# A relative-bias scratch of 23 copies instead of 128, and its skewed read in the weights' queue

## The chip, the cores and the metric

The kernel runs on one core of a Trainium2 chip. The metric is the device time of one execution in microseconds; the median over the runs counts. TensorE (PE), VectorE (DVE), ScalarE (ACT) and GpSimd (POOL) compute, SyncE (SP) issues transfers, and 16 DMA engines move the data, whichever engine issued them.

## The reference, cut to what matters

Two transformer blocks run one behind the other on 256 tokens of width 1024, all in float32. The first block has two layers (mixer, memory cross-attention, convolutional feed-forward). The second has one layer, and its attention adds a bias that depends on the head and on the distance of query and key alone:

```python
d = jnp.maximum(dist, 0)                         # dist = query - key
large = max_exact + (jnp.log(df / max_exact) / math.log(...) * (REL_BUCKETS - max_exact)).astype(jnp.int32)
bucket = jnp.where(d < max_exact, d, jnp.minimum(large, REL_BUCKETS - 1))
...
bias_gr = rel_bias.T.reshape(G, R, REL_BUCKETS)
s_c = einsum("bgrqd,bgcd->bgrqc", qb, kc) + bias_gr[:, :, t5_bucket(tq[:, None] - cend[None, :])]
s_s = einsum("bgrqd,bgqld->bgrql", qb, k_sel) + bias_gr[gi5, ri5, t5_bucket(dist_s)[:, :, None]]
s_w = einsum("bgrqd,bgsd->bgrqs", qb, kwb) + bias_gr[:, :, t5_bucket(dist_w)]
```

There are 16 heads. Since only the distance counts, a head's bias over keys is the same row of numbers for each query, shifted by one place from query to query.

## The kernel before

**Weights.** Nearly all of the work is products with weights, which are read once. They lie in memory in the order of use, cut into pieces of up to 128 x 1024; two equal neighbours make a group (`grouped`), mostly 1024 KB. SyncE runs one loop over the groups (`sync`, L2343 to L2351): group `gi` goes into slot `gi % NR` of a ring of `NR` = 4, and its issue waits until the products have used all pieces of group `gi - 4` (`product`, "used"). ScalarE casts each piece to its high part (`highs`, L998), VectorE subtracts to get the low part (`lows_due`, L1494), both up to 3 pieces ahead of the product, in the order of their programs; TensorE then multiplies high and low parts (`run`, L477). So a group that lands late makes ScalarE wait, then VectorE, then TensorE.

**The first place: the write of the scratch.** While the feed-forward of the first block's first layer runs, TensorE and VectorE make the 16 heads' bias rows, 384 numbers each, in partitions 0 to 15 of `PT`. GpSimd then writes each row 128 times into the scratch `d_scr` in memory (L2276, behind the eighth of its 22 products of that stage). Its signal is `bias_out`.

**The second place: the skewed read.** Partition p of the table `TB` (128 partitions x 16 heads x 256 keys) needs a head's row from place 127 - p on. A step of 383 from one partition to the next, over copies that stand 384 apart, gives that shift. GpSimd issues the read (L2303, signal `bias_in`) once the first block's last operations no longer need the space of `TB` (`first_block_done`: the last normalisation, and the last of the products "dn"). VectorE is the only reader: first for the compressed keys (L2041), later for each unit of the attention.

**The weights around the second place.** The second block begins with two products for the queries ("q2", 0 and 1), then two for keys and values ("kv2", 0 and 1), 4 pieces each, so two groups each. The first of them is computed by row tile (`tokens_by_tile`): tile 0, then tile 1, and a piece counts as used only after tile 1. The groups of "kv2" 0 are issued when the groups of "q2" 0 are free, those of "kv2" 1 when the groups of "q2" 1 are.

Of the kernel before, what the change touches and what calls it, by code (L numbers as in the profile page):

```python
# [25 lines left out]
NR = 4  # L26
# [205 lines left out]
def build(nc, wstream, specs_out, cst_d, rel_d, par_d, par2_d, x_d, xT_d, memT_d, lnp_d, scr_d, out_d, layout):  # L232
    with ExitStack() as ctx:

        def sb(name, f):
            return ctx.enter_context(nc.sbuf_tensor(name, [128, f], F32))
# [4 lines left out]
        def signal(name, step=1):  # L241
            s = Signal(ctx.enter_context(nc.semaphore("s_" + name)), step)
            signals.append(s)
            return s
# [3 lines left out]
        product = signal("product")  # L248
# [4 lines left out]
        vec = signal("vec")  # L253
# [3 lines left out]
        cst_in, x_in, p2_in, rel_in, mem_in, bias_out, bias_in = (  # L257
            signal(n, 16) for n in ("cst", "x", "p2", "rel", "mem", "bias_out", "bias_in"))
# [16 lines left out]
        PT = sb("PT", 2048)  # L275
# [26 lines left out]
        def arena(n):  # L302
            o = at[0]
            at[0] += n
            assert at[0] <= ARENA
            return ar[:, o:o + n]
# [35 lines left out]
        def pr(name, p=128):  # L342
            o, n = layout["par"][0][name]
            return par[0:p, o:o + n]
# [11 lines left out]
        q2 = arena(2048).rearrange("p (f t) -> p f t", t=T)  # L356
        kT2 = arena(1024).rearrange("p (b f t) -> p b f t", b=2, t=T)
        TB_o = at[0]
        TB = arena(4096).rearrange("p (h s) -> p h s", s=T)
# [55 lines left out]
        pieces = Pieces()  # L415
# [1070 lines left out]
        def vector(e):  # L1486
            w = Waits(e)
# [538 lines left out]
            for i in range(2):  # L2026
# [5 lines left out]
                bc = TB[:, :, first:first + 16 * (ncv - 1) + 1:16]  # L2032
                b3 = A["csc", i][:, 0:240].rearrange("p (h c) -> p h c", c=NC15)
                w.wait_ge(cross, "csc", i)
                w.wait_ge(bias_in)
                if i:
                    w.wait_ge(cross, "pT2", 0, 6, 0)
                    w.wait_ge(cross, "pT2", 0, 7, 0)
# [153 lines left out]
        def gpsimd(e):  # L2192
            w = Waits(e)

            def inverse_root(dst, src, n=1, p=128):
                w.wait_ge(cst_in)
                return e.tensor_tensor(dst, src, mhalf[0:p, 0:n], ALU.pow)  # L2197
# [6 lines left out]
            def scaled(tag, *ready):  # L2204

                w.wait_ge(*ready)
                for i in range(2):
                    e.tensor_scalar(xt(i), xt(i), ALPHA, None, ALU.mult).then_inc(*pool.done("scaled", *tag, i))

            def roots(tag):  # L2210

                for i in range(2):
                    st, mv, nm, ve_, rs, nr = norm_smalls(i)
                    w.wait_ge(vec, "var", *tag, i)
                    inverse_root(rs, ve_).then_inc(*pool.done("rs", *tag, i))
# [6 lines left out]
            for l in range(DEPTH):  # L2222
                scaled((l, 1), *((x_in,) if l == 0 else (cross, "xT", 0, 3, 1, 1)))

                def rope_sin(br, i):
                    Xv = qk[:, i, 640 * br:640 * br + 640].rearrange("p (h s d) -> p h s d", s=2, d=32)
                    t2v = room[br][:, 640:1280].rearrange("p (h s d) -> p h s d", s=2, d=32)
                    n1 = rot[:, br, i, 32:64].unsqueeze(1).to_broadcast([128, 10, 32])
                    if i:
                        w.wait_ge(vec, "rope", l, br, 0)  # L2230
                    e.tensor_tensor(t2v[:, :, 0, :], Xv[:, :, 1, :], n1, ALU.mult).then_inc(*pool.done("sin", l, br, i))

                w.wait_ge(cst_in)
                if l:
                    for n in range(NZ - 4, NZ):
                        w.wait_ge(pool, "z", 0, n)
                        w.wait_ge(vec, "z", 0, n)
                for i in range(2):
                    w.wait_ge(act, "q", l, 0, i)
                    w.wait_ge(act, "k", l, i)  # L2240
                    rope_sin(0, i)
                for i in range(2):
                    w.wait_ge(vec, "vvar", l, i)
                    inverse_root(sm[:, 32 * i + 15:32 * i + 16], sm[:, 32 * i + 14:32 * i + 15]).then_inc(*pool.done("vrs", l, i))
                    w.wait_ge(vec, "qvar", l, i)
                    inverse_root(sm[:, 84:94], sm[:, 74:84], 10).then_inc(*pool.done("qrs", l, i))
                    if i == 0:
                        w.wait_ge(vec, "qg", l, 0)
                        rope_sin(1, 0)
                    w.wait_ge(act, "vn", l, i)  # L2250
                    w.wait_ge(par_in[l])
                    e.tensor_tensor(vt[:, i, :], vt[:, i, :], pr("clng"), ALU.mult).then_inc(*pool.done("vgain", l, i))
                    w.wait_ge(pool, "vgain", l, i)
                    e.tensor_tensor(vt[:, i, :], vt[:, i, :], pr("clnb"), ALU.add).then_inc(*pool.done("vn", l, i))
                w.wait_ge(vec, "qg", l, 1)
                rope_sin(1, 1)
                for kind, n, d in fills:
                    if kind == "merge" and n != 2:
                        w.wait_ge(vec, "mul", l, n, d)
                        w.wait_ge(*((vec, "mul", l, 2, d) if n == 0 else (pool, "merged", l, 0, d)))  # L2260
                        e.tensor_tensor(merged[:, d, :], merged[:, d, :], gates[:, gate_at[n] + d, :],  # L2261
                                        ALU.add).then_inc(*pool.done("merged", l, n, d))
                roots((l, 1))
                next_gains((l, 1), 3 * l + 1, (l, 2))
                scaled((l, 2), cross, "xT", l, 1, 1, 1)
                roots((l, 2))
                next_gains((l, 2), 3 * l + 2, (l, 3))
                scaled((l, 3), cross, "xT", l, 2, 1, 1)
                for n in range(NZ):
                    s = 2 * n % 8  # L2270
                    w.wait_ge(act, "ga", l, n)
                    w.wait_ge(vec, "conv", l, n + NZ)
                    e.tensor_tensor(hc[:, s, :], hc[:, s, :], hc[:, s + 1, :], ALU.mult).then_inc(*pool.done("z", l, n))  # L2273
                    if l == 0 and n == 7:
                        w.wait_ge(vec, "rel")
                        e.dma_start(scr_d, PT[0:16, 1024:1408].unsqueeze(1).to_broadcast([16, 128, 384])).then_inc(*bias_out.done())  # L2276
                if l == 0:
                    w.wait_ge(vec, "conv", 0, 2 * NZ - 1)
                    e.dma_start(par, par_d[1]).then_inc(*par_in[1].done())
                else:  # L2280
                    for n in range(NZ - 4, NZ):
                        w.wait_ge(pool, "z", 1, n)
                        w.wait_ge(vec, "z", 1, n)
                    e.dma_start(grow, lnp_d[6][:, 0:1024]).then_inc(*gain_in[2, 1].done())
                roots((l, 3))
                if l == 0:
                    next_gains((0, 3), 3, (1, 1))
# [4 lines left out]
                    w.wait_ge(vec, "rvar", *tag, i)  # L2292
                    inverse_root(rs, ve_).then_inc(*pool.done("rrs", *tag, i))

            def first_block_done():
                for i in range(2):
                    w.wait_ge(vec, "ln", 1, 3, i, 1)
                w.wait_ge(product, "dn", 1, 1, 1)

            rms((2, 1))  # L2300
            w.wait_ge(bias_out)
            first_block_done()
            e.dma_start(TB, bass.AP(scr_d.tensor, 127, [[383, 128], [128 * 384, 16], [1, 256]])).then_inc(*bias_in.done())  # L2303
            for i in range(2):
                w.wait_ge(vec, "qv", i)
                inverse_root(ve[i][:, 48:72], ve[i][:, 24:48], 24).then_inc(*pool.done("qrs2", i))
# [1 line left out]
            def keys_scaled(i):  # L2308
                Xh = qb[:, i, :].rearrange("p (h d) -> p h d", d=64)
                w.wait_ge(vec, "qsc", i)  # L2310
                w.wait_ge(p2_in)
                for h, name in ((16, "ksn"), (20, "kwn")):
                    e.tensor_tensor(Xh[:, h:h + 4], Xh[:, h:h + 4], p2(name).unsqueeze(1).to_broadcast([128, 4, 64]),
                                    ALU.mult).then_inc(*pool.done("qn", i))
# [2 lines left out]
            w.wait_ge(vec, "kve")  # L2317
            inverse_root(krs, kve, 1, 60).then_inc(*pool.done("krs"))
            keys_scaled(1)
            e.memset(up[0:RP, :, 0:3], 0.0).then_inc(*pool.done("pad"))  # L2320
            for i in range(2):
                for un in range(8):
# [18 lines left out]

        def sync(e):
            w = Waits(e)  # L2343
            for gi, (at, p, f) in enumerate(pieces.source):
                if gi >= NR:
                    for n in pieces.groups[gi - NR]:
                        w.wait_ge(product, "used", n)
                elif gi:
                    w.wait_ge(xT_in[3])
                o = gi % NR * RAW  # L2350
                e.dma_start(raws[0:p, o:o + f], bass.AP(wstream.tensor, at, [[f, p], [1, f]])).then_inc(*ring_in[gi % NR].done(gi))  # L2351
            w.wait_ge(out_done, 1, 1)


# [155 lines left out]
```

## Time and profile before

| what | us |
|---|---|
| median of 3 runs | 1654.6 |
| lowest and highest run | 1652.38 and 1656.0 |
| the profiled execution | 1651.64 |
| its span, first to last instruction | 1649.8 |
| TensorE busy in the span | 1555.0 |
| VectorE busy | 1032.8 |
| ScalarE busy | 794.6 |
| GpSimd busy | 233.6 |

The profile is of one execution, so its times add up to 1651.64, not to the median. Busy time says little by itself; what is read below is where TensorE waits, for what, and what the DMA engines do at that time. Times of rows are microseconds from the start of the span.

### The profile page before, as it was taken

The page shows a single profiled execution, that of the slowest core. Times are in us where ns is not written, and L with a number is a line of the kernel's source. Part 1 is how long each engine was busy: PE and PEld are TensorE (multiplying, and loading weights), DVE is VectorE, ACT ScalarE, POOL GpSimd, SP SyncE. Part 2 cuts the span into 40 slices and gives each one's busy share as a digit, 9 for nine tenths or more (in the row PEclk, how much of TensorE's full clock was granted, in tenths as well). Part 3 has the DMA queues.
Part 4 walks back from the last instruction along what each step waited for, and adds up shares of the span by engine and source line. Part 5 has one row for each costly group of instructions (what it writes and reads, how often), then busy time and mean ns, then how long its engine had stood idle before and what let it go on. Part 6 is the DMA issues. An engine that isn't in the chain of part 4 may idle for free.

```text
span 1649.8 us, 25273 instructions
## 1 busy us (share of the span) xinstructions
PE 1555.0 (94%) x10399; PEld 1401.1 (85%) x10399; DVE 1032.8 (63%) x1704; ACT 794.6 (48%) x1423; POOL 233.6 (14%) x189
## 2 busy tenths in 40 slices
PE   9999999798998999989889999899988799989999
PEld 6899889698986889989689986697876699979987
DVE  5765585675856675477668865455654486546643
ACT  4545355364643555444356652453446564435531
POOL 2300121211202120032031100012010040100000
PEclk9989999899999999999989999899999899989999
DMA  8533355359564533255345554455211244535553
GB/s 314 225 103 105 101 207 201 115 179 208 189 220 159 201 125 127 79 179 204 125 153 183 179 195 175 158 182 185 90 44 52 73 154 152 199 115 189 182 180 126
DMA packets 41027, 261.32 MB, mean 158 GB/s; under 512 B 4513, under 2 KB 5153, under 8 KB 14673
## 3 DMA queue, kind: packets, MB, share of 16 engines
q1 hardware_dynamic: 35600, 238.44, 42.0%
q0 software_dynamic: 2944, 15.69, 3.7%
q10 hardware_dynamic: 2368, 5.58, 0.9%
q8 instruction: 82, 1.34, 0.3%
q14 instruction: 33, 0.26, 0.0%
HBM read 254.98 MB, written 4.19 MB: 157 GB/s over the span
## 4 chain that ended last, share of the span: by engine, by line
PE 78%; DVE 10%; ACT 4%; issue 3%; DMA 3%; POOL 1%; ACTq 0%; DVEq 0%; POOLq 0%; SPq 0%
PE ps L477 69%; PE ps L583 3%; DMA raw<-d_wst 3%; DVE lows L1494 2%; PE ps L664 1%; ACT S L1406 1%; ACT wh L998 1%; DVE ar L2015 1%; PE ps L685 1%; POOL sm L2197 1%; DVE S L2077 1%; PE ps L579 1%; PE ps L703 1%; PE ps L702 0%; ACT xTr L1019 0%
## 5 line engine op out<-in xcount | busy, mean ns | idle before, releaser
L1494 DVE TENSOR_TENSOR lows<-raw,wh 128x1024 fp32r<-128x1024 f32 (+3 forms) x473 | 545.4, 1171 | 254.1 <-ACT wh L998 251.8
L477 PE MATMUL ps<-xTr,wh 128*128 128x256 f32 (+2 forms) x3664 | 674.0, 286 | 13.8 <-DVE lows L1494 9.2
L477 PEld LDWEIGHTS ps<-xTr,wh 128*128 128x128 f32 (+2 forms) x3664 | 574.6, 192 | 19.2 <-issue 14.9
L998 ACT CAST wh<-raw 128x1024 fp32r<-128x1024 f32 (+3 forms) x473 | 455.7, 989 | 192.1 <-DMA raw<-d_wst 153.9
L477 PE MATMUL ps<-xTr,lows 128*128 128x256 f32 (+2 forms) x1832 | 522.1, 285 | 0.0
L477 PEld LDWEIGHTS ps<-xTr,lows 128*128 128x128 f32 (+2 forms) x1832 | 352.3, 192 | 0.0
L477 PE MATMUL ps<-wh,arR 128*128 128x512 f32 x928 | 296.7, 398 | 4.7 <-DVE ar L1660 3.9
L477 PEld LDWEIGHTS ps<-wh,arR 128*128 128x128 f32 x928 | 175.2, 189 | 49.4 <-DVE ar L1660 5.7
L477 PE MATMUL ps<-lows,arR 128*128 128x512 f32 x464 | 184.2, 397 | 0.0
L477 PE MATMUL ps<-arR,wh 128*128 128x256 f32 (+1 forms) x832 | 148.4, 281 | 0.0
L477 PE MATMUL ps<-wh,xTr 128*128 128x512 f32 x384 | 122.4, 398 | 8.3 <-DVE xTr L1513 3.1
L477 PEld LDWEIGHTS ps<-arR,wh 128*128 128x128 f32 (+1 forms) x832 | 127.2, 188 | 0.2
L477 PE MATMUL ps<-arR,lows 128*128 128x256 f32 (+1 forms) x416 | 116.3, 280 | 0.0
L477 PEld LDWEIGHTS ps<-lows,arR 128*128 128x128 f32 x464 | 87.5, 189 | 20.3
L2197 POOL TENSOR_TENSOR sm<-sm,cst 128x1 f32<-128x1 f32 (+3 forms) x27 | 43.9, 1627 | 413.3 <-DVE sm L1535 265.2
L477 PEld LDWEIGHTS ps<-wh,xTr 128*128 128x128 f32 x384 | 73.6, 192 | 26.4 <-DVE lows L1494 4.1
L477 PEld LDWEIGHTS ps<-arR,lows 128*128 128x128 f32 (+1 forms) x416 | 78.2, 188 | 0.0
L477 PE MATMUL ps<-lows,xTr 128*128 128x512 f32 x192 | 76.0, 396 | 0.0
L1233 ACT ACTIVATE S<-ps,ar 128x256 f32<-128x256 f32 x88 | 49.4, 561 | 51.1 <-PE ps L477 51.1
L2273 POOL TENSOR_TENSOR S<-S 128x256 f32<-128x256 f32 x44 | 42.1, 958 | 221.8 <-ACT S L1215 200.0
L2261 POOL TENSOR_TENSOR ar<-ar 128x256 f32<-128x256 f32 x32 | 31.9, 996 | 233.9 <-DVE ar L1660 233.8
L1019 ACT CAST xTr<-ps 128x512 fp32r<-128x512 f32 x28 | 15.5, 590 | 84.1 <-PE ps L583 83.9
(260 smaller groups left out, 1551.0 us busy)
## 6 DMA issues: line engine op xcount, KB each, us to landing
raw<-d_wst SPq DMA_DIRECT2D x196, 1024.0 KB, 4.9
raw<-d_wst SPq DMA_DIRECT2D x24, 512.0 KB, 3.5
raw<-d_wst SPq DMA_DIRECT2D x12, 896.0 KB, 4.6
raw<-d_wst SPq DMA_DIRECT2D x8, 672.0 KB, 4.6
ar<-d_lnp POOLq DMA_DIRECT2D x5, 1024.0 KB, 5.1
raw<-d_wst SPq DMA_DIRECT2D x8, 441.0 KB, 3.5
d_scr<-PT POOLq DMA_DIRECT2D x1, 3072.0 KB, 36.1
ar<-d_par POOLq DMA_DIRECT2D x2, 1192.0 KB, 9.5
```

Of the source, the lines that this page charges most:

```text
L477: op = e.matmul(out, s, m, start=start and i == 0, stop=stop and i == len(pairs) - 1)
L579: e.matmul(b[:, :], ident, cst("wmask"), start=True, stop=True)
L583: op = e.transpose(o, x, ident[0:x.shape[0], 0:x.shape[0]])
L664: op = e.matmul(b[:, h * 64:(h + 1) * 64], PTv[:, hold + h, k, :], va[:, k, v:v + 64], start=(k == 0), stop=(k == 1))
L685: op = e.matmul(bv[:, k, :], qT[br][lo:lo + 64, 2 * hh + k, i * 128:(i + 1) * 128], kT[br][lo:lo + 64, :], start=True, stop=True)
L703: op = e.matmul(bv[:, gg, :], ones[:, 0:128], bs[:, gg * 128:(gg + 1) * 128], start=False, stop=True)
L998: e.copy(high_of(m), raw_of(m)).then_inc(*high.done(m))
L1233: e.activation(hc[:, s, :], M["up", l, m][:, 0:T], ACT.Identity, bias=cb[:, m:m + 1], scale=ck[:, m, 1:2]).then_inc(*act.done("h", l, m))
L1494: e.tensor_tensor(low_of(m), raw_of(m), high_of(m).bitcast(F32), ALU.subtract).then_inc(*low.done(m))
L2197: return e.tensor_tensor(dst, src, mhalf[0:p, 0:n], ALU.pow)
L2261: e.tensor_tensor(merged[:, d, :], merged[:, d, :], gates[:, gate_at[n] + d, :], ALU.add).then_inc(*pool.done("merged", l, n, d))
L2273: e.tensor_tensor(hc[:, s, :], hc[:, s, :], hc[:, s + 1, :], ALU.mult).then_inc(*pool.done("z", l, n))
```

## The change

The scratch keeps 23 copies of each head's row. The read becomes sixteen transfers: number `a` fills the partitions 8a to 8a + 7, for which it reads copies a to a + 7 (8a rows of 383 are a rows of 384 and a shift of 376a; the highest copy read is 15 + 7). They are issued by SyncE, behind the group of weights `second`, which is the one whose slot the last group of "q2" 0 leaves. The waits for the first block's end stand ahead of them, and once more on GpSimd ahead of the memset of the pad of `up`. VectorE waits for all sixteen.

```diff
-                w.wait_ge(bias_in)
+                w.wait_ge(bias_in, 15)
...
-                        e.dma_start(scr_d, PT[0:16, 1024:1408].unsqueeze(1).to_broadcast([16, 128, 384])).then_inc(*bias_out.done())
+                        e.dma_start(scr_d, PT[0:16, 1024:1408].unsqueeze(1).to_broadcast([16, 23, 384])).then_inc(*bias_out.done())
...
-            def first_block_done():
-                for i in range(2):
-                    w.wait_ge(vec, "ln", 1, 3, i, 1)
-                w.wait_ge(product, "dn", 1, 1, 1)
-
             rms((2, 1))
-            w.wait_ge(bias_out)
-            first_block_done()
-            e.dma_start(TB, bass.AP(scr_d.tensor, 127, [[383, 128], [128 * 384, 16], [1, 256]])).then_inc(*bias_in.done())
...
             keys_scaled(1)
+            for i in range(2):
+                w.wait_ge(vec, "ln", 1, 3, i, 1)
+            w.wait_ge(product, "dn", 1, 1, 1)
             e.memset(up[0:RP, :, 0:3], 0.0).then_inc(*pool.done("pad"))
...
+            second = pieces.home[pieces.of["q2", 0][-1]][0] + NR
             for gi, (at, p, f) in enumerate(pieces.source):
...
                 e.dma_start(raws[0:p, o:o + f], bass.AP(wstream.tensor, at, [[f, p], [1, f]])).then_inc(*ring_in[gi % NR].done(gi))
+                if gi == second:
+                    w.wait_ge(bias_out)
+                    for i in range(2):
+                        w.wait_ge(vec, "ln", 1, 3, i, 1)
+                    w.wait_ge(product, "dn", 1, 1, 1)
+                    for a in range(16):
+                        e.dma_start(TB[8 * a:8 * a + 8], bass.AP(scr_d.tensor, 127 + 376 * a, [[383, 8], [23 * 384, 16], [1, 256]])
+                                    ).then_inc(*bias_in.done(a))
...
-    scr = dram("scr", [16, 128, 384], "Internal")
+    scr = dram("scr", [16, 23, 384], "Internal")
```

The order of the other engines' instructions stays as it is. On SyncE before, from the second layer's weights to the gates of the second block (`raw` is the ring, `d_wst` the weights in memory; 128x384 is the small group of the attention's gates, which follows "kv2" 1):

```order
L2351 DMA raw<-d_wst 128x1024 [waits s_product] x12
L2351 DMA raw<-d_wst 128x2048 [waits s_product] x53
L2351 DMA raw<-d_wst 128x384 [waits s_product]
L2351 DMA raw<-d_wst 128x2048 [waits s_product] x2
L2351 DMA raw<-d_wst 128x1792 [waits s_product] x2
```

And with the change:

```order
L2347 DMA raw<-d_wst 128x1024 [waits s_product] x12
L2347 DMA raw<-d_wst 128x2048 [waits s_product] x51
L2354 DMA ar<-d_scr 8x16x256 [waits s_vec,s_bias_out]
L2354 DMA ar<-d_scr 8x16x256 x15
L2347 DMA raw<-d_wst 128x2048 [waits s_product] x2
L2347 DMA raw<-d_wst 128x384 [waits s_product]
```

The sixteen reads (`ar` is the memory of `TB`) stand ahead of the last two groups before the gates, the two of "kv2" 1. On GpSimd before, at the start of the second block:

```order
L2197 TENSOR_TENSOR sm<-sm,cst 128x1 [waits s_vec] x4
L2303 DMA ar<-d_scr 128x16x256 [waits s_product,s_bias_out]
L2197 TENSOR_TENSOR sm<-sm,cst 128x24 [waits s_vec] x2
L2313 TENSOR_TENSOR ar<-ar,par 128x256 [waits s_p2,s_vec]
L2320 MEMSET ar 112x12x3
```

And with the change:

```order
L2197 TENSOR_TENSOR sm<-sm,cst 128x1 [waits s_vec] x4
L2197 TENSOR_TENSOR sm<-sm,cst 128x24 [waits s_vec] x2
L2305 TENSOR_TENSOR ar<-ar,par 128x256 [waits s_p2,s_vec]
L2197 TENSOR_TENSOR sm<-sm,cst 60x1 [waits s_vec]
L2315 MEMSET ar 112x12x3 [waits s_product]
```

The read has left that queue with its waits, and the memset has got the wait for the last product of the first block.

## Rows read from the trace of the kernel before

**Rows 1.** The page: span, busy time by engine, and the chain's shares by engine.

```profile
span 1649.8 us, 25273 instructions
PE 1555.0 (94%) x10399; PEld 1401.1 (85%) x10399; DVE 1032.8 (63%) x1704; ACT 794.6 (48%) x1423; POOL 233.6 (14%) x189
PE 78%; DVE 10%; ACT 4%; issue 3%; DMA 3%; POOL 1%; ACTq 0%; DVEq 0%; POOLq 0%; SPq 0%
```

**Rows 2.** Timeline of GpSimd, 370 to 377 us: start, us, engine, line, operation.

```profile
373.52 1.10 POOL L2276 DMA_DIRECT2D d_scr<-PT  x1
```

**Rows 3.** DMA issues of the whole span: count, KB each, median us to landing.

```profile
raw<-d_wst SPq DMA_DIRECT2D x196, 1024.0 KB, 4.9
...
d_scr<-PT POOLq DMA_DIRECT2D x1, 3072.0 KB, 36.1
...
ar<-d_scr POOLq DMA_DIRECT2D x1, 2048.0 KB, 9.4
```

**Rows 4.** DMA queues, 380 to 385 us: packets, MB, share of 16 engines.

```profile
DMA packets 111, 0.51 MB, mean 102 GB/s; under 512 B 0, under 2 KB 0, under 8 KB 111
...
q0 software_dynamic: 111, 0.51, 97.5%
```

**Rows 5.** The chain of waits, 380 to 430 us: start, us, what.

```profile
377.69 22.30 DMA raw<-d_wst
...
400.02 1.05 ACT wh L998
...
401.09 1.24 DVE lows L1494
...
402.46 10.44 PE ps L477 x72
```

**Rows 6.** Waits of TensorE, 370 to 420 us: total, times, longest.

```profile
PE ps L477 <- DVE lows L1494: 7.6, 1, 7.6
```

**Rows 7.** Busy time by stretch, behind the pause; PEclk stands after POOL.

```profile
402.40:405.00 2.60, 2.54 (x12) 2.57 (x13) 1.90 (x4) 1.81 (x3) 0.50 (x1) 0.50 1.04 267
405.00:407.50 2.50, 2.50 (x19) 2.50 (x19) 1.42 (x3) 0.16 (x1) 0.00 (x0) 0.80 0.97 231
```

**Rows 8.** Timeline of SyncE's queue, 383 to 429 us, issues of groups.

```profile
383.45 0.33 SPq L2351 DMA_DIRECT2D raw<-d_wst  x1
...
394.97 0.33 SPq L2351 DMA_DIRECT2D raw<-d_wst  x1
...
421.99 0.33 SPq L2351 DMA_DIRECT2D raw<-d_wst  x1
...
427.75 0.33 SPq L2351 DMA_DIRECT2D raw<-d_wst  x1
```

**Rows 9.** DMA queues, 1036 to 1045 us.

```profile
q0 software_dynamic: 528, 2.10, 73.5%
```

**Rows 10.** Timeline of VectorE, 1150 to 1185 us: the first reader of the table.

```profile
1159.36 0.35 DVE L2041 TENSOR_TENSOR S<-ps,ar 128x112 f32<-128x112 f32 x1 [1.66 <-PE ps L895]
```

**Rows 11.** Timeline of GpSimd, 1000 to 1200 us: the operation behind the read's issue.

```profile
1108.44 9.12 POOL L2197 TENSOR_TENSOR sm<-sm,cst 128x24 f32<-128x24 f32 x2 [71.93 <-DVE sm L1930]
```

**Rows 12.** The line of the weights' issues: duration ns, least, median, most.

```profile
L2351 SPq DMA_DIRECT2D raw<-d_wst x249: 312/328/432, 0.7 to 1624.3; - x125
```

**Rows 13.** Timeline of SyncE's queue, 1053 to 1077 us.

```profile
1054.30 0.33 SPq L2351 DMA_DIRECT2D raw<-d_wst  x1
...
1059.74 0.33 SPq L2351 DMA_DIRECT2D raw<-d_wst  x1
...
1076.07 0.33 SPq L2351 DMA_DIRECT2D raw<-d_wst  x1
```

**Rows 14.** DMA queues and issues, 1060 to 1065 us.

```profile
q1 hardware_dynamic: 144, 1.05, 62.2%
...
raw<-d_wst SPq DMA_DIRECT2D x1, 1024.0 KB, 4.8
```

**Rows 15.** The chain of waits, 1060 to 1085 us.

```profile
1059.89 25.16 PE ps L477 x111
```

## The prediction

> **What bounds the kernel now.** I read the page first. TensorE is busy for 1555.0 of a span of 1649.8 us, and the chain that ended last lies on it for 78% [rows 1]. So a change that touches only transfers can win or lose time only where TensorE stands still because weights came late, and I looked for such places at the two transfers that the change touches.
>
> *The write of the scratch.* GpSimd issues it at 373.52 us [rows 2], and it lands 36.1 us later, where a group of weights of 1024 KB takes 4.9 us in the median [rows 3]. Between 380 and 385 us every byte that moved belongs to the write's queue: 0.51 MB in 5 us, 102 GB/s, with the engines of the DMA 97.5% taken [rows 4]. The weights' queue does not appear in that answer at all. The local chain shows what this costs: the group issued at 377.69 lands after 22.30 us, is cast (1.05 us) and split by VectorE (1.24 us), and only then, at 402.46, does TensorE go on [rows 5]. It had stood for 7.6 us [rows 6]. After the pause its granted clock is 0.50 in the first 2.6 us, half of full speed (1.2 of 2.4 GHz), and 0.80 in the next 2.5 us [rows 7].
>
> The whole cost is read from the weights' queue, which issues a group whenever TensorE has used one. Before the pause the beat is 5.76 us (383.45 minus 377.69), and behind it again 5.76 (427.75 minus 421.99). The third issue after the one at 394.97 should come at 394.97 + 3 x 5.76 = 412.25 and comes at 421.99 [rows 5, 8]. **The write costs 9.74 us**: 7.6 of standing and 2.1 of slow clock.
>
> *The skewed read.* GpSimd's read lands 9.4 us after its issue [rows 3] and moves 2.10 MB with the engines of the DMA 73.5% taken over 9 us, that is 6.6 us at full use [rows 9]. The weights' queue has nothing in that answer: it stands still there, because the first second-block product frees its weights only at its second row tile. So the read costs the weights nothing now. Its reader on VectorE, L2041, starts at 1159.36 [rows 10], over 100 us later.
>
> **The change part by part.** *The smaller write* moves 23/128 of 3072 KB, 552 KB. At the 102 GB/s of [rows 4] that is 5.5 us, so it is over at about 381 us. The group issued at 377.69 then lands at 381 + 4.9 = 386 at the latest. TensorE needs it in place by the time it ran dry less the cast and the split: 402.46 - 7.6 - 2.5 = 392.4. There are 6 us to spare, so the whole 9.74 us should go. I take **-9.7 us**; the bounds are -9.74 and, if the write still held the weights back as long as now, 0.
>
> *GpSimd's queue* loses one wait and one issue, ahead of an operation that waits 71.9 us for VectorE anyway [rows 11]: nothing. The wait for the first block's end goes to the memset of the pad, long after that end: nothing. In SyncE's queue the three waits ahead of the reads are met, because the group issued just before needed weights freed by the first product of the second block, which comes later than all three: nothing.
>
> *The sixteen issues on SyncE.* One issue takes 0.328 us, in the median of 249 [rows 12]; 16 of them are 5.2 us. They follow the issue at 1054.30, so they end at 1059.9, where the next group is issued at 1059.74 today [rows 13]. Delay 0.1 us, hidden. If an issue took twice that, the group would go out 5 us later, which the slack below still covers.
>
> *What now stands ahead of that group.* In one queue the groups land one behind the other, so I let it land behind the 2.10 MB of reads. Call X the time that the reads take. A group there lands 4.8 us after its issue, the one of 1054.30 so at 1059.1 [rows 13, 14]. The next one then lands at 1059.1 + X + 3.1, the last number being its own moving time (62.2% of 5 us, [rows 14]). Cast, split and gaps take 2.5 us, as in [rows 5]. TensorE begins with it when it has used up the group before, which is when the queue issues again: 1076.07 [rows 13]. So TensorE stands for 1059.1 + X + 3.1 + 2.5 - 1076.07 = **X - 11.4 us**, and nothing as long as X is under 11.4. That it is fully busy there, 25.16 us in one piece, shows that nothing else covers a wait [rows 15]. A long one also brings the slow clock, another 2.1 us as in the first stage.
>
> *How long is X?* No row has a transfer onto 8 partitions. From below: the read as it is, 6.6 us [rows 9], over 128 partitions at once. From above: the write, whose SBUF side is 16 partitions, gets 102 GB/s while alone [rows 4]; if the rate goes with the partitions that are open, 8 of them get 51 GB/s and 2.10 MB take 41 us. The new transfers look more like the second row: every one of them has all its bytes in 8 neighbouring partitions. But there all engines stay on the same 16 partitions to the end, while here an engine that is ahead goes on to the next transfer's partitions, so that the crowding loosens. I take **28 us**, two thirds of the upper bound.
>
> Then TensorE stands for 16.6 us and loses 2.1 to the clock: **+18.7 us**. With the write's 9.7 that is **+9.0 us**. The profiled execution took 1651.64 us (span 1649.8) and would take 1660.6; it lies 3.0 us under the median of 1654.6, so the forecast for the median is **1663.6 us**.
>
> Two rules of the Trainium skill bear on X. The page "SBUF — State Buffer", section "Door 1: The DMA port swizzle", says that a transfer's bandwidth goes with the ports that its partitions reach, and gives 104 GB/s for partitions 0 to 15; the 102 GB/s of the write agree. By it 8 partitions reach two ports of about 27 GB/s, an estimate of 39 us for X and +20 us for the change. The page "DMA: Bandwidth & Descriptors", section "Why a DMA increments its semaphore by 16 and not by 1", says that a transfer is split over the largest number up to 16 that divides the slowest dimension of both sides; that would be 8 engines here, and no run so far shows it.
>
> **The rivals.**
>
> *The reads run nearly as fast as the one they replace* (faster). If the partitions that are open set no limit to a write into SBUF, X is 6.6 us, or 13.2 if each transfer, with its 8 partitions, keeps only half of the 16 engines busy. For it: [rows 4] shows a read out of SBUF, not a write into it, and the 16 transfers stand in the queue together, so engines could spread over several of them. Against it: the nearest row in shape is the slow one. With X of 6.6 nothing stands, -9.7: 1644.9 us. With 13.2 TensorE stands for 1.8: 1646.7. The sign turns at X - 11.4 + 2.1 = 9.7, X = 19.
>
> The second of these two times is also what the page on DMA would give by its rule of the engine count alone.
>
> *The two parts cancel.* X between 16 and 22, about halfway between the bounds: TensorE stands for 5 to 11 us, and the time is within 3.3 us of before, 1654.6.
>
> *The write is not relieved* (the change doesn't do what it says). If what holds the weights back is not the number of bytes, the -9.7 are missing and the forecast becomes 1673. Against it: the write's rate is the same steady 102 GB/s that gives its 36 us.
>
> **How the numbers follow.** A difference under 0.2%, 3.3 us, can hardly be told from none. The forecast (X from 22 to 41, the write relieved) has 0.57; reads at speed 0.27; cancelling 0.13; the write unrelieved 0.03. Faster is therefore 0.27, same 0.13, slower 0.57 + 0.03 = 0.60. Within the forecast X = 22 gives 1657.6 and X = 41 gives 1676.6, its own range. The range that holds 8 in 10 must take in the fast rival, since that has more than 2 in 10: from 1643 (1644.9 less half the spread of the runs, 1.8) to 1674 (X = 38), which leaves out the slowest reads, part of the last rival and little else.
>
> **What would show it.** Right: the write lands within some 10 us, no pause of TensorE near 395, and the weights' beat stays at 5.76 us there; then a pause of some 17 us about 10 us before today's 1076, on weights of which the group behind the reads takes some 30 us to land instead of 4.8, and the clock at 0.5 after it. Wrong: no such pause, reads that land within 13 us of the first, and a time near 1645. A pause left at 395 would speak for the third rival. Issues of SyncE much over 0.33 us would be a cost that I put at nothing.

## The result, and the profile after

| | before | with the change |
|---|---|---|
| median, us | 1653.49 (4 runs) | 1668.2 (4 runs) |
| lowest and highest | 1651.93, 1656.0 | 1665.55, 1669.79 |
| profiled execution | 1651.64 | 1669.23 |
| its span | 1649.8 | 1667.4 |

The ratio is 1.0092, with a 95% interval of 1.0073 to 1.011: the change makes the kernel slower by 12 to 18 us. The forecast was 1663.6, 9.0 us above the 1654.6 that it started from; the medians here are 14.7 us apart, the profiled executions 17.6.

**The first place came out as forecast.** The write among the DMA issues of the changed kernel (count, KB, us to landing), and the beat of SyncE's queue after it:

```profile
d_scr<-PT POOLq DMA_DIRECT2D x1, 552.0 KB, 7.7
```

```profile
388.73 0.33 SPq L2347 DMA_DIRECT2D raw<-d_wst  x1
394.49 0.33 SPq L2347 DMA_DIRECT2D raw<-d_wst  x1
400.25 0.33 SPq L2347 DMA_DIRECT2D raw<-d_wst  x1
406.01 0.33 SPq L2347 DMA_DIRECT2D raw<-d_wst  x1
```

The write lands in 7.7 us instead of 36.1 [rows 3], and the beat of 5.76 us goes through where [rows 8] have the gap. TensorE's waits between 360 and 420 us are an empty list. When the second block's weights are reached, the group that was issued at 1054.30 [rows 13] goes out at 1044.57: 9.73 us have been won.

**At the second place more was lost.** The chain of waits of the changed kernel, 1030 to 1130 us:

```profile
1037.13 28.40 PE ps L477 x117
1065.54 23.30 DMA raw<-d_wst
1088.86 1.05 ACT wh L998
...
1089.93 1.24 DVE lows L1494
...
1091.22 18.94 PE ps L477 x96
```

It has the shape of [rows 5]. The first group of "kv2" 1 was issued at 1065.54 and landed 23.30 us later, and TensorE went on at 1091.22. Its waits between 1000 and 1150 us:

```profile
PE ps L477 <- DVE lows L1494: 25.4, 2, 25.0
```

One wait of 25.0 us. The kernel before has only the other one there, of 0.4 us. In the table of stretches TensorE's busy time, PEld, DVE, ACT and POOL are followed by its granted clock, the DMA share and GB/s:

```profile
1066.00:1091.00 25.00, 0.25 (x2) 0.00 (x0) 1.06 (x1) 1.99 (x2) 0.00 (x0) 0.55 0.98 151
1091.00:1095.00 4.00, 3.78 (x9) 3.04 (x10) 3.05 (x4) 3.65 (x8) 0.00 (x0) 0.50 0.30 126
```

After the pause the clock is again at its lower level, 0.50, for some 4 us. Downstream nothing else moves: the first reader of the table, L2041, starts at 1177.20 instead of 1159.36 [rows 10], so 17.84 us later. That is -9.73 from the first place and +27.6 from the second: 25.0 of standing, and 2.6 that are left for the slow clock. The granted clock gives nearly as much, an estimate: 4.0 us at 0.50 and, in the same table, 3.0 us at 0.87 (1095 to 1098) lose 2.4 us together. The two profiled executions differ by 17.6.

What the DMA engines did meanwhile, in the changed kernel's queues from 1050 to 1055 us, when the reads were alone (packets, MB, rate; then the queue's share of 16 engines):

```profile
DMA packets 319, 0.31 MB, mean 61 GB/s; under 512 B 21, under 2 KB 319, under 8 KB 319
...
q1 hardware_dynamic: 319, 0.31, 57.1%
```

The reads move 61 GB/s, where the read that they replace had 2.10 MB in 6.6 us at full use [rows 9], about 320 GB/s. And they keep little more than half of the 16 engines busy. (The share reads somewhat high: rows below reach 117%.) The count of packets says the same. The weights' queue before, and with the change:

```profile
q1 hardware_dynamic: 35600, 238.44, 42.0%
```

```profile
q1 hardware_dynamic: 37776, 240.54, 43.3%
```

That is 2176 more, 136 for each of the sixteen reads. 128 of these are the pieces of 1 KB, and I read the 8 that are left as the end of the transfer, one for each engine that takes part; a group of weights has 144 for its 128 rows, so 16. The Trainium skill's page "DMA: Bandwidth & Descriptors", section "Why a DMA increments its semaphore by 16 and not by 1", gives the count of engines as the largest number up to 16 that divides the slowest dimension of both sides. The 8 seen here agree with it.

SyncE's issues were not what I took them for. Line L2354, the sixteen reads (duration in ns, least, median, most; first and last start):

```profile
L2354 SPq DMA_DIRECT2D ar<-d_scr x16: 275/1072/3390, 1045.0 to 1063.5; - x16
```

They took from 1045.0 to 1065.4, 20.4 us instead of 5.2, so that the group behind them went out 15 us after the time forecast for it.

Once it was out, weights and reads moved at the same time. Queues from 1070 to 1075 us:

```profile
DMA packets 289, 0.56 MB, mean 112 GB/s; under 512 B 16, under 2 KB 250, under 8 KB 250
...
q1 hardware_dynamic: 289, 0.56, 111.3%
```

250 of the packets are under 2 KB, 16 of these under 512 B; the other 234 are pieces of 1 KB. So the reads were down to about 48 GB/s, and about 0.3 MB of weights passed beside them. In the packets of the trace the pieces of 1 KB run from 1048.7 to 1085.3 us, 36.6 us in all; the group landed 3.5 us later, at 1088.84.

### The profile page after: what moved, and what is told of

The parts are those of the page before. It is cut to its first block, busy times and chain, and to the rows that moved or that the text cites. A ratio compares the mean times of both kernels' runs of the same rounds, so it can differ in the third digit from the quotient of the medians.

```text
span 1667.4 us, 25288 instructions
## 1 busy us (share of the span) xinstructions
PE 1552.5 (93%) x10399; PEld 1397.7 (84%) x10399; DVE 1034.0 (62%) x1704; ACT 795.2 (48%) x1423; POOL 224.1 (13%) x188
## 3 DMA queue, kind: packets, MB, share of 16 engines
q1 hardware_dynamic: 37776, 240.54, 43.3%
## 4 chain that ended last, share of the span: by engine, by line
PE 76%; DVE 10%; ACT 5%; issue 4%; DMA 3%; POOL 1%; ACTq 0%; POOLq 0%; DVEq 0%; SPq 0%
PE ps L477 68%; PE ps L583 3%; DMA raw<-d_wst 3%; DVE lows L1494 2%; ACT wh L998 1%; PE ps L664 1%; DVE ar L2015 1%; ACT S L1406 1%; POOL sm L2197 1%; PE ps L685 1%; DVE S L2077 1%; PE ps L703 0%; PE ps L759 0%; PE ps L702 0%; PE ps L741 0%
## 5 line engine op out<-in xcount | busy, mean ns | idle before, releaser
L477 PEld LDWEIGHTS ps<-xTr,wh 128*128 128x128 f32 (+2 forms) x3664 | 572.5, 192 | 11.5 <-issue 6.8
L2273 POOL TENSOR_TENSOR S<-S 128x256 f32<-128x256 f32 x44 | 35.3, 803 | 219.6 <-ACT S L1215 219.6
```

The costliest lines, as they stand in the source:

```text
L477: op = e.matmul(out, s, m, start=start and i == 0, stop=stop and i == len(pairs) - 1)
```

## The experiments

After the result three readings were left. **P**: the partitions decide; bytes that go to a few neighbouring partitions crowd, on top of which an outer size of 8 leaves half of the engines out. **N**: pieces of 1 KB on half of the engines are slow, whatever the partitions. **I**: SyncE is 20 us late with sixteen issues, and that holds the weights. Besides them: does the move into the weights' queue cost anything by itself, and is the write's term right? The edits of e_spread, e_wide16, e_move_only and e_four32 are shown against the changed kernel, the others against the kernel before; hunks that only fit the number of copies or of signals are left out (`...`).

**The same sixteen reads over partitions that stand apart** (run e_spread).

```diff
                     for a in range(16):
-                        e.dma_start(TB[8 * a:8 * a + 8], bass.AP(scr_d.tensor, 127 + 376 * a, [[383, 8], [23 * 384, 16], [1, 256]])
+                        p0 = 32 * (a // 4) + a % 4
+                        e.dma_start(TB[p0:p0 + 29:4], bass.AP(scr_d.tensor, 127 - p0, [[380, 8], [23 * 384, 16], [1, 256]])
                                     ).then_inc(*bias_in.done(a))
```

> The sixteen reads stay in SyncE's queue with the same bytes and the same copies, but each one fills 8 partitions that stand 4 apart instead of 8 neighbours. Theory P (neighbouring partitions crowd the same way into the memory): the reads take about 13 us (twice the 6.6 us of the old read, since half of the DMA engines take part), TensorE stands for about 2 us instead of 25.0, and the time is 1653.5 - 9.7 + 2 = about 1646. Rival N (each transfer keeps half of the engines and its small pieces are slow whatever partitions they go to): nothing changes, 25 us of standing, about 1668. Rival I (SyncE needs 20 us to issue sixteen transfers, and that alone holds the weights): nothing changes, about 1668, with issues of over 1 us each.

Measured: 1648.08 us, ratio to before 0.9972 (0.996 to 0.9985), faster than before and 20 us faster than the change; P had about 1646 and 2 us of standing. Queues from 1050 to 1055 us, and TensorE's waits from 1030 to 1092:

```profile
DMA packets 971, 0.94 MB, mean 188 GB/s; under 512 B 58, under 2 KB 970, under 8 KB 970
...
q1 hardware_dynamic: 970, 0.93, 54.2%
```

```profile
PE ps L477 <- DVE lows L1494: 3.0, 2, 2.6
```

Same bytes, same size of the pieces, same queue, same number of transfers, and the same 37776 packets, so still half of the engines (54.2%). The rate is 188 GB/s instead of 61, and the longest wait 2.6 us instead of 25.0. N has fallen, and so has I in its first form: sixteen issues now took 11.5 us (0.65 us each in the median), so their length in the changed kernel went with the crowding. One thing differs besides the partitions: these reads take only the first 8 of the 23 copies, where the change's transfer `a` takes copies a to a + 7. That the place in memory makes the difference is unlikely: the reads of 128 partitions are fast from 128 copies (run e_move_only, landing in 10.4 us) and from a single one (run e_write_only, 10.0 us).

**Twice as many neighbours in each read** (run e_wide16).

```diff
...
-                    for a in range(16):
-                        e.dma_start(TB[8 * a:8 * a + 8], bass.AP(scr_d.tensor, 127 + 376 * a, [[383, 8], [23 * 384, 16], [1, 256]])
+                    for a in range(8):
+                        e.dma_start(TB[16 * a:16 * a + 16], bass.AP(scr_d.tensor, 127 + 368 * a, [[383, 16], [23 * 384, 16], [1, 256]])
                                     ).then_inc(*bias_in.done(a))
...
```

> Eight reads of 16 neighbouring partitions instead of sixteen of 8, same bytes, same 23 copies, same place in the queue. P: 16 neighbours let 102 GB/s through, as in the old write, so the reads take about 20 us, TensorE stands for about 9 and loses 2 to the clock: 1653.5 - 9.7 + 11 = about 1655. N: all 16 engines take part, the reads take about 7 us and nothing stands: 1644. I: half as many issues, so half of the standing, about 12 us: about 1658, and the pause ends when the issues do.

Measured: 1652.65 us, ratio 1.0 (0.9986 to 1.0014). Queues from 1050 to 1055 us, and TensorE's waits from 1030 to 1092:

```profile
DMA packets 622, 0.60 MB, mean 120 GB/s; under 512 B 38, under 2 KB 622, under 8 KB 622
...
q1 hardware_dynamic: 622, 0.60, 116.9%
```

```profile
PE ps L477 <- DVE lows L1494: 7.2, 1, 7.2
```

Now all engines are taken, and still only 120 GB/s come through, fewer than the 188 of half the engines over partitions that stand apart: engines that have work are not engines that move. Twice the neighbours, and with them twice the engines, give twice the rate (61 to 120); what each of the two gives by itself, this run does not tell. P's 9 us of standing were 7.2. The eight issues were over after 4.2 us, and the group behind them went out on time; from the chain of waits:

```profile
1050.59 20.99 DMA raw<-d_wst
```

So here the reads alone make TensorE stand, without any late issue, which is the end of I. The time is that of before, as the gain of the write and this standing with its slow clock cancel: what the prediction listed as its second rival, made on purpose.

**The move alone** (run e_move_only): 128 copies, and the old read in one transfer, in SyncE's queue.

```diff
...
-                    for a in range(16):
-                        e.dma_start(TB[8 * a:8 * a + 8], bass.AP(scr_d.tensor, 127 + 376 * a, [[383, 8], [23 * 384, 16], [1, 256]])
-                                    ).then_inc(*bias_in.done(a))
+                    e.dma_start(TB, bass.AP(scr_d.tensor, 127, [[383, 128], [128 * 384, 16], [1, 256]])).then_inc(*bias_in.done())
...
```

> The write of 128 copies as before, and the old read of 128 partitions in one transfer, but in SyncE's queue at the place of the sixteen. P: 2.10 MB ahead of the weights take about 7 us, under the 11.4 that the ring covers, so nothing changes at the second place, and the write's pause near 395 us is back: 1653.5, as before. Rival M (any 2 MB ahead of the weights make TensorE wait there): a pause near 1076 us and 1658 or more.

Measured: 1651.53 us, ratio 0.9995 (0.9983 to 1.0007): no change. TensorE's waits in 360 to 420 us show the write's pause as in [rows 6]; in 1040 to 1092 us there is no wait for VectorE's low parts. The read lands 10.4 us after its issue.

```profile
PE ps L477 <- DVE lows L1494: 8.0, 1, 8.0
```

Rival M falls: 2.10 MB ahead of the weights cost nothing here, where they pass in less than the 11.4 us that the ring covers.

**The small write alone** (run e_write_only).

```diff
-                        e.dma_start(scr_d, PT[0:16, 1024:1408].unsqueeze(1).to_broadcast([16, 128, 384])).then_inc(*bias_out.done())
+                        e.dma_start(scr_d, PT[0:16, 1024:1408].unsqueeze(1).to_broadcast([16, 23, 384])).then_inc(*bias_out.done())
...
-            e.dma_start(TB, bass.AP(scr_d.tensor, 127, [[383, 128], [128 * 384, 16], [1, 256]])).then_inc(*bias_in.done())
+            e.dma_start(TB, bass.AP(scr_d.tensor, 127, [[0, 128], [23 * 384, 16], [1, 256]])).then_inc(*bias_in.done())
...
```

> The small write alone: 23 copies, and one read of 128 partitions by GpSimd at the old place. The read takes one unshifted row for all partitions, so the bias is not skewed in this kernel; bytes and pieces are those of the old read. All theories: the pause near 395 us is gone, none appears near 1066, 1653.5 - 9.7 = about 1643.8. If the write's relief were worth less than its term, the time would lie above 1647.

Measured: 1643.17 us, ratio 0.9945 (0.9924 to 0.9966), 9.9 us between the medians. TensorE has no wait between 360 and 420 us. The write's term of 9.74 stands.

**Reads that use all engines and do not crowd** (run e_four32): 32 copies, four reads of 32 partitions each, 4 apart, where the sixteen stood.

```diff
...
-                    for a in range(16):
-                        e.dma_start(TB[8 * a:8 * a + 8], bass.AP(scr_d.tensor, 127 + 376 * a, [[383, 8], [23 * 384, 16], [1, 256]])
+                    for a in range(4):
+                        e.dma_start(TB[a:a + 125:4], bass.AP(scr_d.tensor, 127 - a, [[380, 32], [32 * 384, 16], [1, 256]])
                                     ).then_inc(*bias_in.done(a))
...
```

> 32 copies, and four reads in SyncE's queue at the place of the sixteen, each over 32 partitions that stand 4 apart. Theory P (neighbouring partitions crowd; an outer size of 8 keeps half of the engines out): all engines take part and at most two of them meet at a time, so the reads take 7 to 10 us, less than the 11.4 that the ring covers: nothing stands, 1653.1 - 9.7 = about 1643.5, faster than both kernels. Rival Q (what counts is 2.10 MB of pieces of 1 KB ahead of the weights, whatever their shape): the standing of 2.6 us of the spread reads stays, about 1648.

Measured: 1643.18 us, ratio 0.9926 (0.9898 to 0.9955). Queues from 1050 to 1055 us:

```profile
DMA packets 1808, 1.80 MB, mean 360 GB/s; under 512 B 50, under 2 KB 1808, under 8 KB 1808
...
q1 hardware_dynamic: 1808, 1.80, 108.6%
```

360 GB/s, and of TensorE's waits for low parts 0.4 us are left, as in the kernel before. This kernel beats both. Q falls. The write of 768 KB lands in 10.0 us and holds nothing back.

**The same reads from GpSimd, at the old place** (run e_four32_pool).

```diff
...
-            e.dma_start(TB, bass.AP(scr_d.tensor, 127, [[383, 128], [128 * 384, 16], [1, 256]])).then_inc(*bias_in.done())
+            for a in range(4):
+                e.dma_start(TB[a:a + 125:4], bass.AP(scr_d.tensor, 127 - a, [[380, 32], [32 * 384, 16], [1, 256]])
+                            ).then_inc(*bias_in.done(a))
...
```

> The same 32 copies and four reads, issued by GpSimd at the old place, when the weights' queue stands still. P: over before the weights go on, no standing at either place, about 1643.5, the same as with the reads in SyncE's queue. If the place in the queue matters by itself, this one is faster than that one.

Measured: 1644.15 us, ratio 0.9928 (0.9906 to 0.995), not to be told from run e_four32. For reads of that shape the place makes no difference that these runs can tell.

**The crowded reads from GpSimd, at the old place** (run e_pool16).

```diff
...
-            e.dma_start(TB, bass.AP(scr_d.tensor, 127, [[383, 128], [128 * 384, 16], [1, 256]])).then_inc(*bias_in.done())
+            for a in range(16):
+                e.dma_start(TB[8 * a:8 * a + 8], bass.AP(scr_d.tensor, 127 + 376 * a, [[383, 8], [23 * 384, 16], [1, 256]])
+                            ).then_inc(*bias_in.done(a))
...
```

> The change's 23 copies and its sixteen reads of 8 neighbours, but issued by GpSimd at the old place, in a queue of their own. Rival F (the reads hurt only because the weights' queue serves them first): the weights pass beside them, and the time is that of the small write, about 1643.5. Theory E (crowded reads hold the DMA engines themselves, as the old write held them from another queue): the reads take about 35 us from 1026 on, the groups issued at about 1042 and 1045 land after 1060 instead of 1047 and 1050, TensorE stands for 8 to 14 us, and the time is 1653 to 1660.

Measured: 1644.65 us, ratio 0.9936 (0.991 to 0.9961): the time that F gave, and E's was missed. The queues from 1040 to 1050 us say why, and they are not F's reason:

```profile
DMA packets 599, 1.00 MB, mean 100 GB/s; under 512 B 360, under 2 KB 360, under 8 KB 595
...
q0 software_dynamic: 595, 0.97, 107.0%
q1 hardware_dynamic: 4, 0.03, 3.6%
...
raw<-d_wst SPq DMA_DIRECT2D x2, 1024.0 KB, 10.1
```

The weights hardly passed beside the reads: their two groups went out at 1044.69 and 1047.44, up to 1050 us only 4 packets of them moved, and they took 10.1 us to land instead of 4.8. So E's mechanism is there. But the reads had started at 1028, they went at 100 GB/s over all 16 engines (107%) instead of 61 over half of them, and they were over by about 1051. The delay of 5 us stayed inside what the ring covers. So it was not that the weights could overtake: the earlier start and the faster pace saved the change. The pace came with GpSimd's queue, in which the bytes also moved in packets of 4 KB (0.97 MB in the 235 packets that are not under 512 B) instead of 1 KB; whether the engines or the packets made it, no run takes apart. So 8 neighbours are not held to 61 GB/s everywhere, and P is shown for SyncE's queue alone.

## Why the prediction was right, and where its size was off

*The write.* Forecast -9.74, measured -9.73 in the issue times and 9.9 between the medians of run e_write_only. The reading of the queue's beat, instead of the wait alone (7.6), was worth it: the slow clock after the pause is in it. One thing in the picture was too simple: the old write did not keep the weights out to its end. The group issued at 377.69 landed at 399.99 [rows 5], ten microseconds ahead of the write itself (373.52 + 36.1); the last section has the rows.

*The standing, X - 11.4.* The form was right: the wait of each run with its reads in SyncE's queue fits it. Taken back from the longest wait, X is 36.4 us in the changed kernel, 14.0 with partitions apart and 18.6 with 16 neighbours. The pieces of 1 KB in the traces of these runs take 36.6, 14.4 and 17.9 us from the first to the last, measured without the wait. In the two runs where they take least (6.5 us in e_four32, 6.3 in e_move_only) nothing stood. The rates seen while the reads were alone, 61, 188 and 120 GB/s, would give 34, 11 and 18 us. In the first two the reads take longer, because the groups do not pass strictly one behind the other, as the sum has it: weights and the rest of the reads moved at the same time, and the reads more slowly, as the rows of the changed kernel from 1070 to 1075 us show.

*The size of X* is the term that was mis-sized: 28 us were forecast, 36.4 came, so that 25.0 us of standing stand against 16.6. The step that failed is the allowance for engines that run ahead into the next transfer's partitions. I had taken a third off the upper bound of 41 us for it, and about a ninth was right: against the bound's 51 GB/s the reads ran at 61 to 71 while alone, and at about 48 beside the weights. No row stood behind the third, and the sign hung on X lying above 19, so that the forecast came out on the right side is in part luck. The slow clock took the 2.6 that are left, against 2.1. Between the profiles 17.6 were seen, between the medians 14.7, and forecast were +9.0.

By the port rule of the Trainium skill (page "SBUF — State Buffer", section "Door 1: The DMA port swizzle") the estimate of X was 39 us, nearer than my own 28. Its table has 104 GB/s measured for partitions 0 to 15, and run e_wide16 shows 120 for reads of 16 neighbours that stand in a queue together. Run e_pool16 does not fit it: 8 neighbours reach two ports, an estimate of 54 GB/s by the rule, and 100 were measured, so the rule for one transfer does not give the rate of several in flight.

*Issues of SyncE.* Put at 0.33 us each and at no cost. They took 20.4 us in all, but nothing shows a cost of their own: the reads went on until 1085.3, 20 us after the group was issued, and in run e_wide16, where the group went out on time, TensorE stood all the same. No run has sixteen crowded reads with quick issues. Uncrowded reads also took longer to issue than a group of weights (0.65 us in the median in run e_spread, 0.69 in e_four32); only the long issues, up to 3.39 us, belong to the crowded ones.

*The rivals.* Reads at full speed: wrong for 8 neighbours, and run e_four32 shows that only their shape kept it from being right (1643.2 measured, 1644.9 in that rival's sum). The two parts cancel: wrong with X at 36.4, and run e_wide16 with X at 18.6 is that case. The write unrelieved: wrong, no pause near 395.

## What to carry to other kernels

When a transfer is cut into several, look at which partitions each piece fills and not at bytes alone: in SyncE's queue 8 neighbours got 61 GB/s, the same bytes over 8 partitions 4 apart 188, over 32 partitions 4 apart 360. Before something is put ahead of a prefetch stream, work out how long the stream can be held before its consumer starves, here 11.4 us; well below that it was free, above it every microsecond was paid, and the slow clock on top. And a change of two parts may be a good one and a bad one: the smaller write alone was worth 9.9 us, and with better-shaped reads the kernel runs at 1643.18, where the kernel before, measured beside it, took 1654.05.

## What the runs showed of the hardware that I had not expected

Two queues do not always share the engines evenly. At the start of the kernel before, from 16 to 20 us, the weights (q1) and GpSimd's loads (q0) move side by side, packet for packet, at 430 GB/s together:

```profile
q1 hardware_dynamic: 125, 0.89, 52.9%
q0 software_dynamic: 125, 0.83, 49.3%
```

Under the crowded old write no weights moved from 380 to 391 us, although the groups issued at 377.69 and 383.45 were waiting ([rows 4] have 5 us of it). After that they moved beside the write, slowly; from 390 to 395 us:

```profile
q0 software_dynamic: 94, 0.43, 70.9%
q1 hardware_dynamic: 66, 0.54, 25.6%
```

In run e_pool16 it was 4 packets between the first issue at 1044.69 and 1050. So the crowded transfers held the other queue for some microseconds, though not to their end; what ends the hold, no run shows.

An issue on SyncE is not of fixed length: 0.33 us for a group of weights, up to 3.39 us for a read while the reads ahead of it crept at 61 to 71 GB/s. SyncE is then itself blocked, and with it every later issue in its program: the group behind the reads went out 15 us late.
